# Sparse attention with its query and output projections woven between the head pairs, and sums of squares taken by piece before the last gated stage

## The reference, cut to what matters

```
qg = h @ w_qg
q = qg[:, :1024] * 64 ** -0.5;  gates = sigmoid(qg[:, 1024:])
o_cmp = softmax(q . k_cmp - slope * distance, visible) . v_cmp     # 15 compressed blocks
o_slc = softmax(q . k_slc - slope * distance, causal) . v_slc      # all 4 blocks are selected here
o_win = softmax(q . k_win - slope * distance, causal) . v_win
x = x + (g0 * o_cmp + g1 * o_slc + g2 * o_win) @ w_o
```

## Time and profile before

| what | value |
|---|---|
| median of 3 runs | 1021.89 us |
| the profiled execution's own time | 1023.04 us |
| its span, first to last instruction | 1021.2 us |
| granted TensorE clock, mean, as a share of full speed | 0.981 |
| PE busy | 976.2 us (96%) |
| DVE busy | 709.1 us (69%) |
| ACT busy | 483.9 us (47%) |
| chain that ended last | PE 82%, DVE 9%, ACT 5%, issue 2%, DMA 1% |

### The profile page before, as it was taken

One profiled execution on the slowest core, in us unless ns is written; L12 is line 12 of the kernel. 1 busy time (PEld: TensorE's weight loads), 2 busy tenths in 40 slices (PEclk: granted clock), 3 DMA queues, 4 the chain that ended last, 5 costly groups with the idle time before them and its releaser, 6 DMA issues.

```text
span 1021.2 us, 19481 instructions
## 1 busy us (share of the span) xinstructions
PE 976.2 (96%) x7934; PEld 945.4 (93%) x7934; DVE 709.1 (69%) x1128; ACT 483.9 (47%) x699; POOL 81.6 (8%) x129
## 2 busy tenths in 40 slices
PE   4999999999999998889999999999999789999998
PEld 4999999999999996569999999999999689999998
DVE  4876777777777646967777777677876466655554
ACT  5344634444445414866434444446757354444441
POOL 6000001000000011330010000011000000000000
PEclk9999999999999978999999999989999899999999
DMA  9655748687745670007668677543444254655531
GB/s 278 197 197 200 255 148 301 233 286 244 249 144 174 202 252 1 1 22 256 199 221 303 232 272 267 164 125 100 149 166 152 76 185 135 237 190 180 184 103 41
DMA packets 131387, 186.98 MB, mean 183 GB/s; under 512 B 6272, under 2 KB 102656, under 8 KB 131328
## 3 DMA queue, kind: packets, MB, share of 16 engines
q1 hardware_dynamic: 123984, 159.82, 47.2%
q0 software_dynamic: 6912, 25.17, 7.1%
q10 hardware_dynamic: 432, 1.16, 0.4%
HBM read 185.09 MB, written 1.05 MB: 182 GB/s over the span
## 4 chain that ended last, share of the span: by engine, by line
PE 82%; DVE 9%; ACT 5%; issue 2%; DMA 1%; SPq 0%; DVEq 0%; ACTq 0%
PE ps L1754 44%; PE ps L1823 15%; PE ps L1750 11%; PE ps L1752 3%; PE ps L1880 1%; DVE ada_acc L1156 1%; PE ps L1790 1%; DVE g_lo L1191 1%; ACT g_hi L703 1%; DMA g_raw<-in_a_w_in 1%; ACT g_hi L640 1%; ACT e_even L829 1%; DVE d_lo L1142 1%; DVE e_even L1436 1%; DVE g_lo L1091 1%
## 5 line engine op out<-in xcount | busy, mean ns | idle before, releaser
L1754 PE MATMUL ps<-opa_hi,g_hi 128*128 128x256 f32 x864 | 250.2, 290 | 14.8 <-DVE opa_lo L1128 11.9
L1754 PE MATMUL ps<-opa_lo,g_hi 128*128 128x256 f32 x864 | 247.3, 286 | 0.0
L1754 PE MATMUL ps<-opa_hi,g_lo 128*128 128x256 f32 x864 | 247.1, 286 | 0.0
L1754 PEld LDWEIGHTS ps<-opa_hi,g_hi 128*128 128x128 f32 x864 | 168.9, 195 | 17.8 <-issue 15.4
L1191 DVE TENSOR_TENSOR g_lo<-g_raw,g_hi 128x2048 fp32r<-128x2048 f32 x54 | 123.8, 2292 | 69.7 <-ACT g_hi L703 69.7
L1754 PEld LDWEIGHTS ps<-opa_lo,g_hi 128*128 128x128 f32 x864 | 168.8, 195 | 0.2
L1754 PEld LDWEIGHTS ps<-opa_hi,g_lo 128*128 128x128 f32 x864 | 168.7, 195 | 0.0
L1091 DVE TENSOR_TENSOR g_lo<-g_raw,g_hi 128x2048 fp32r<-128x2048 f32 x59 | 135.2, 2291 | 47.0 <-ACT g_hi L640 46.5
L640 ACT ACTIVATE g_hi<-g_raw 128x2048 fp32r<-128x2048 f32 x59 | 112.6, 1909 | 93.0 <-PE ps L1754 80.4
L1823 PE MATMUL ps<-hid_hi,d_hi 128*128 128x256 f32 x528 | 147.8, 280 | 1.5 <-issue 1.4
L1823 PE MATMUL ps<-hid_hi,d_lo 128*128 128x256 f32 x528 | 147.5, 279 | 0.0
(11 more groups left out here) (313 smaller groups left out, 1848.5 us busy)
## 6 DMA issues: line engine op xcount, KB each, us to landing
g_raw<-in_f_w_gu SPq DMA_DIRECT2D x44, 1024.0 KB, 8.9
ada_raw<-in_w_ada POOLq DMA_DIRECT2D x48, 512.0 KB, 5.2
d_raw<-in_f_w_down SPq DMA_DIRECT2D x22, 1024.0 KB, 5.2
g_raw<-in_w_in SPq DMA_DIRECT2D x14, 1024.0 KB, 7.8
g_raw<-in_w_gate SPq DMA_DIRECT2D x11, 1024.0 KB, 7.1
g_raw<-in_w_up SPq DMA_DIRECT2D x11, 1024.0 KB, 9.6
d_raw<-in_w_down SPq DMA_DIRECT2D x11, 1024.0 KB, 5.1
g_raw<-in_a_w_in SPq DMA_DIRECT2D x10, 1024.0 KB, 8.0
```

Of the source, the lines that this page charges most:

```text
L1754: mm = pe.matmul(pair(b)[:, a, :], wt[:, a * P:(a + 1) * P], xt, **st)
```

## The change

Query steps QG+2 and QG+3 and the output steps WO and WO+1 are cut into slices ("units") of six matmuls, and stand between the PE work of the head pairs. So `opb_hi` and `opb_lo` have to live through the attention, and `e_even` and `pt_buf` move to memory over the second half of `ada_acc`. Banks change: QG+2, QG+3 and WO use bank 6; the transposes of a pair rotate through banks 4 and 5 alone; the small products and `ada_sum(0)` use bank 7. The compressed attention is done in two halves of eight heads, the second one at pair 3. `ada_sum(0)` is cut in four and stands in front of `values(2)` to `values(5)`. DVE makes the low parts of QG+3 and WO, and takes the queries of QG+2 and QG+3, inside the attention. On ACT the high part of WO goes ahead of the exponentials of pair 3, and that of WO+1 ahead of those of pair 7. Ahead of the third feed-forward stage the squares are added piece by piece, all before the split of F2+1, and a Silu of two columns stands behind the root.

```diff
     def gbank(g):
-        return 4 + g % 4
+        return 6 if g in (QG + 2, QG + 3, WO) else 4 + g % 4
...
@@ ACT
             root((1, 3, 6)[f])
+            if f == 2:
+                act.activation(small[:, 12:14], eps[:, 0:2], ACT.Silu)
             split_g(g0 + 3)
...
-            split_g(WO)
...
+            compressed_exp(0)
             for j in range(1, NH // 2 + 2):
+                if j == 3:
+                    split_g(WO)
+                if j == 5:
+                    compressed_exp(1)
                 if j < NH // 2:
                     exps(j, 0)
...
-                        act.activation(pt_buf[:, 512 * q:512 * q + 512], ps[:, 4 + q, :], ACT.Copy).then_inc(pt_copied, 1)
+                        act.activation(pt_buf[:, 512 * q:512 * q + 512], ps[:, 4 + q % 2, :], ACT.Copy).then_inc(pt_copied, 1)
...
+                if j == 6:
+                    split_g(WO + 1)
...
+            squares(6, 3)
             split_g(F2 + 1)
-            squares(6, 3)
@@ DVE
             shift(0)
             shift(1)
+            own(dve.tensor_scalar(gates[:, :, :], gates[:, :, :], 1.0, None, ALU.add))
+            own(dve.reciprocal(gates[:, :, :], gates[:, :, :]))
+            compressed_shift(0)
             normalize(0)
             normalize(1)
...
+            compressed_factors(0)
+            evac_q(2)
+            split_g(QG + 3)
             for j in range(2, NH // 2 + 2):
                 for e in range(2):
                     if j < NH // 2 + 1:
                         normalize(2 * j - 2 + e)
+                    if j == 3 and e == 0:
+                        split_g(WO)
+                    if j == 4 and e == 0:
+                        evac_q(3)
                     if j < NH // 2:
                         shift(2 * j + e)
+                if j == 5:
+                    compressed_factors(1)
...
+                if j == 4:
+                    compressed_shift(1)
+                if j == 8:
+                    split_g(WO + 1)
...
+                if s in (2, 3):
+                    add_squares(6, (s - 1,))
+            add_squares(6, (3,))
             split_g(F2 + 1)
-            add_squares(6)
@@ PE
+            scores(0)
+            query_units(0, 2)
+            compressed_scores(0)
+            query_units(2, 1)
...
+            def turn(j, e):
...
+                        q = i // 4
+                        if i % 4 == 0 and (j >= 1 or q == 2):
+                            pe.wait_ge(pt_copied, 3 * j + 1 if q == 2 else 3 * j - q)
+                        mm = pe.transpose(ps[:, 4 + q % 2, i % 4 * P:(i % 4 + 1) * P], x[:, lo:lo + P], ident[:, :])
...
+                if 2 <= j < 6:
+                    ada_sum(0, 6 * (j - 2), 6)
...
+            scores(1)
+            pe.wait_ge(cs_shift, 1)
+            query_units(3, 2)
+            turn(0, 0)
+            query_units(5, 1)
+            turn(0, 1)
+            query_units(6, 2)
...
+            scores(2)
+            compressed_turn(0)
+            query_units(8, 1)
+            values(0)
+            query_units(9, 1)
+            turn(1, 0)
+            query_units(10, 1)
+            turn(1, 1)
+            query_units(11, 1)
...
+            out_units(0, 0, 2)
+            values(6)
+            out_units(0, 2, 1)
+            turn(7, 0)
+            out_units(0, 3, 1)
+            turn(7, 1)
+            out_units(0, 4, 2)
+            values(7)
+            out_units(0, 6, 1)
+            out_units(1, 0, 2)
+            out_units(0, 7, 1)
+            out_units(1, 2, 6)
+            for s in (2, 3):
+                g_step(WO + s, opa_hi, opa_lo, no_wait)
```

More of the change, by code:

```diff
@@ L175, in layer_kernel @@
     over = ExitStack()
+    sb("pad_e", [P, 3 * D], on=over)
+    e_even = sb("e_even", [P, 2, 768], on=over)
+    pt_buf = sb("pt_buf", [P, 1536], on=over)
+    over.close()
+    over = ExitStack()
     qk_a = sb("qk_a", [P, KT, T], on=over)
@@ L1926, in _ @@
             g_step(QG + 1, opb_hi, opb_lo, no_wait)
-            pe.wait_ge(gate_exp, 1)
-            for a in range(TT):
-                mm = pe.transpose(ps[:, 3, 256 + 48 * a:304 + 48 * a], gate_row[:, a * P:(a + 1) * P], ident[0:48, 0:48])
-            mm.then_inc(gate_turned, 1)
+            pe.wait_ge(g_evac, evacs(KV + 5))
             pe.wait_ge(cmp_hid_silu, 3)
@@ L1968, in values, with query_units @@
-            def values(j):
+            pe.wait_ge(gate_exp, 1)
+            for a in range(TT):
+                mm = pe.transpose(ps[:, 6, 256 + 48 * a:304 + 48 * a], gate_row[:, a * P:(a + 1) * P], ident[0:48, 0:48])
+            mm.then_inc(gate_turned, 1)
+            def query_units(first, n):
+                for u in range(first, first + n):
+                    s, k = QG + 2 + u // KT, u % KT
+                    if u == 0:
+                        pe.wait_ge(gates_copied, 1)
+                    if u == KT:
+                        pe.wait_ge(g_evac, evacs(QG + 2))
+                    g_step(s, opb_hi, opb_lo, no_wait, ks=range(k, k + 1))
@@ new lines, in out_units @@
+            def out_units(s, first, n):
+                for k in range(first, first + n):
+                    if s == 0 and k == 0:
+                        pe.wait_ge(pct_made, 2)
+                    if s == 1 and k == 0:
+                        pe.wait_ge(pt_copied, PT_NSA)
+                    g_step(WO + s, opa_hi, opa_lo, a_filled("attn"), ks=range(k, k + 1))
+            scores(0)
+            query_units(0, 2)
+            pe.wait_ge(kc_made, 4)
+            pe.wait_ge(g_evac, evacs(QG + 1))
@@ L1984, in values @@
                               start=False, stop=True, skip_group_check=True).then_inc(pv_done, 1)
-            for j in range(NH // 2 + 1):
-                if j + 1 < NH // 2:
-                    scores(j + 1)
-                if j == 0:
-                    pe.wait_ge(cs_shift, 1)
-                if j == 1:
-                    pe.wait_ge(cs_made, 1)
-                    for q in range(2):
-                        for a in range(TT):
-                            mm = pe.transpose(ps[:, 7, (2 * q + a) * P:(2 * q + a + 1) * P],
-                                              ctmp[:, a * T + q * P:a * T + (q + 1) * P], ident[:, :])
-                    mm.then_inc(pct_done, 1)
-                if j >= 1:
-                    values(j - 1)
-                if j < NH // 2:
-                    turn(j)
@@ new lines, in _ @@
+            turn(1, 1)
+            query_units(11, 1)
+            scores(3)
+            query_units(12, 2)
+            values(1)
+            query_units(14, 1)
+            turn(2, 0)
+            query_units(15, 1)
+            turn(2, 1)
+            pe.wait_ge(g_evac, evacs(QG + 2))
+            scores(4)
+            values(2)
+            turn(3, 0)
+            pe.wait_ge(g_evac, evacs(QG + 3))
+            compressed_scores(1)
+            turn(3, 1)
+            scores(5)
+            values(3)
@@ new lines, in _ @@
+            turn(4, 0)
+            turn(4, 1)
+            for j in (5, 6):
+                scores(j + 1)
+                if j == 5:
+                    compressed_turn(1)
+                values(j - 1)
+                turn(j, 0)
+                turn(j, 1)
+            out_units(0, 0, 2)
[7 more added lines that the diff above has]
+            out_units(0, 6, 1)
```

159 lines of the change are left out of this document (75 added, 84 removed).

## The result

The changed kernel takes 1013.70 us, the median of six runs (1011.51 to 1017.82), against 1022.12 us of the kernel before in the same session (1021.70 to 1026.34). The ratio is 0.9916, with a 95% interval of 0.9897 to 0.9935: faster by 8.6 us by the ratio (8.4 by the medians), where the forecast had said 14.9 and 1007.0 us, with 1002.5 to 1013.0 as its range. So the sign was right, the gain was put too high by 6.3 us, and the time lies 0.7 us above the range.

The account below looks back on a forecast made before the run. PE, busy 976.2 of 1021.2 us, was taken as the bound, with DVE bounding the attention's steady pairs; 11.0 us from the attention and 3.9 from the third stage made 14.9, giving 1007.0 us, range 1002.5 to 1013.0.

Parts of the forecast that it names:

- (a) to (c): Attention, first scores at 369.15 to DVE's loop at 389.1: one 3.1 us PE wait, one clock fall; lead 18.0.
- (d): Attention, DVE's loop from normalize(2) to normalize(14): 35.9 for six laps plus 8.5 of new work, 44.4 us; lead 10.7.
- (e): Attention's tail on PE, behind the copy at 434.0: 28.8 us, to 462.8, against 30.8 before; lead 12.2.
- handing over: Attention, some 15 new PE waits between engines: 0 to 3 us, taken as 1.2.
- third stage: Start of the third feed-forward stage: squares added earlier gain 2.6 us, earlier table load 1.3; 3.9 us together.
- PE keeps up: Attention, DVE's loop: PE's work there sums to 39.8 us, within the loop's 44.4.
- without slack: Behind the attention: WO+2's low part is ready as PE gets there, with no time to spare.
- the attention's 11.0 us: Whole attention: gain after its lead of 12.2 us less 1.2 for handing over.
- the second fall: Rival, attention pair 2: another clock fall behind PE's 1.7 us wait, 2.3 us on the path, 1009.3 us; chance 0.20.
- Two banks: Rival, attention pairs: turns wait for ACT's first copy, laps 9 us instead of 7.4, 1016.6 us; chance 0.06.
- The squares: Rival, third feed-forward stage: squares bring nothing because the additions delay the last piece, 1010.9 us; chance 0.06.
- fall in every pair: Rival, attention pairs: eight clock falls of 3.3 us, slower than before at 1026.9 us; chance 0.04.

Follow-up runs that it names:

- WO sooner: Changed kernel with ACT's high part of WO one pair earlier, ahead of pair 2's exponentials instead of pair 3's; 1008.78 us, 0.9866 of before.
- sums at the front: Changed kernel with the 24 column sums back in one block ahead of the compressed keys' products; 1018.49 us, 0.9956 of before.
- copy first: Changed kernel with ACT's copy of turn 0's first bank ahead of exps(1, 0) instead of behind it; 1010.69 us, 0.9877 of before.
- the three moves: Changed kernel with copy first, WO sooner and WO+1 sooner together; 1006.98 us, 0.9841 of before; second set 1007.63 us, 0.9849.
- WO+1 sooner: Changed kernel with ACT's high part of WO+1 between pair 4's first and second copy, not ahead of exps(7, 0); 1012.76 us, 0.9902 of before.
- sums in the wait: The three moves with 12 of 24 column sums put into PE's wait for QG+3's low part, the others in pairs 3 and 5; 1005.21 us, 0.9830 of before.

## Why the forecast was right in sign and too large

By its own steps, with the first profile of the changed kernel:

| step | forecast us | measured us |
|---|---|---|
| (a) to (c): first scores (370.40) to DVE's loop | 19.95 | 19.83 |
| (d): DVE's loop | 44.4 | 46.83 |
| (e), handing over included: to the end of WO+3 | 30.5 | 29.17 |
| third stage | gain 3.9 | gain 3.78 |

**(a) to (c) held**, with the mechanism named: the wait for ACT's copy (3.1 forecast, 2.85 measured), one fall of the clock behind it, QG+2's queries and the low part of QG+3 as DVE's last work ahead of the loop.

**(d) was too short by 2.4 us.** The wait for WO's high part is 2.95 and its low part 2.29, together 0.6 more than the 4.6 of the sum. The other terms (queries 0.68, compressed shift 1.25, factors 1.50) fit. What the sum lacked are three waits of 0.67, 0.93 and 0.95 us on PE and ACT (2.55; the six laps themselves took some 0.6 us less than the 35.9), of which the last hangs on WO+1's high part ahead of pair 7's exponentials. The sum had taken PE's total, 39.8, as proof that PE keeps up; it does so on average, and is late at single places. "WO sooner" shows that the wait for WO could have been spared: ACT stood idle one pair earlier.

**(e) was too long by 1.3**: the 1.2 us for handing over were not paid, and WO+2 waits 0.21 us, as "without slack" had it (the view puts this down to issue; the low part ends at 454.51, WO+2 begins at 454.61). So the step sums come out within 1.0 us (95.83 against 94.85), and the profile with neither the fall at QG nor the second one has a stretch of 117.84, where 128.37 less 11.0 is 117.37.

**What failed is the attention's 11.0 us: its base, and the falls of the clock.** The sum was made against one execution, and corrected by 1.15 us for the difference of the totals. In that execution the first fall behind QG+3, is longer than in the four other profiles of before; its stretch is 1.6 us over the mean of five. It made up for that elsewhere (its way from 523.20 to F2 at 822.47 takes 299.3 us, 300.6 in the second profile), so that its total was near the median while the stretch that the change removes was not. And the second fall, a rival with 0.20 at 2.3 us, came in three of six profiles; together with the fall at QG, which is on both sides, the changed kernel's mean lies 2.5 us over its best profile. From 11.0 that leaves 11.0 - 1.6 - 2.5 - 0.5 = 6.4, where 0.5 is what the steps themselves were out by (117.84 against 117.37), and the means give 6.5. This takes one difference apart and does not prove it again; the times do, with 5.7.

**The argument against the second fall was wrong in the forecast's own trace.** It was that PE would wait 1.7 us there, less than the 2.21 after which the clock fell. The same trace has a wait of 1.72 us at the first values, which the earlier trace rows leave out, and behind it a clock of 0.50, in the window that the earlier trace rows leave out:

```profile
409.64 2.83 PE L1979 MATMUL ps<-pt_buf,v_tok 128*64 128x256 f32 x16 [1.72 <-ACT gu L853]
```

```profile
409.75:413.05 3.30, 3.30 (x20) 2.25 (x20) 2.83 (x13) 1.80 (x8) 1.58 (x2) 0.50 0.00 0
```

The values take 2.83 us there in place of 1.52, and 2.08 to 2.83 in all five profiles of before. So a fall behind 1.7 us had been seen, and 0.20 was too little for it.

**The other rivals.** Two banks do not hold up the pairs: behind the first turn PE's waits for the copies are 0.25 to 0.91 us, and from the first shift of one lap to that of the next (402.79, 409.50, 417.26, 424.53, 431.60) DVE's loop takes 6.7 to 7.8 us, not 9. The squares do bring their part, 2.4 us; the 3.9 that the forecast put on this rival has the table load in it. The clock does not fall in every pair: 1.00 in the window from 408 to 414. The Trainium skill ("TensorE: Matmul & The Clock Gate", A second HAM failure mode) would have had it swing with the many short idle times between groups of matmuls; these runs show laps with such waits at 1.00, and single falls: behind waits of 2.85 to 2.87 or 2.51 to 2.53 us in each of the eleven profiles that have one, behind one of 1.61 to 1.64 and then 0.33 us in four of nine (three of the six of the changed attention, and sums at the front), and three times behind one of 0.84 or 0.85 (copy first, the second profile of the three moves, the changed kernel's third).

**One kernel's clock falls in one run and not in another.** The same scores behind the same waits of 1.61 and 0.33 us took 1.49, 2.57 and 2.27 us in the table above. The Trainium skill ("TensorE: Matmul & The Clock Gate", What's actually happening) states the like for the start of a kernel: the number of slow matmuls there is not the same in each run. The table shows it in the middle of one.

The forecast's own test, "the sum is wrong if the loop on DVE takes clearly more than 44 us, or if the clock is below 1.00 for more than one stretch", named both failures of the changed kernel. That its base might be off by as much, it did not ask.

## What to carry to other kernels

Where an engine's clock can fall in one run and not in the next, a stretch that a change removes is read from several profiles, or its steps are priced at the full clock and the falls apart; a total that is near the median says nothing on the stretch. Before a fall is argued away by the length of a wait, every wait of the trace at hand is held against the clock behind it. When work is moved into a loop that another engine bounds, ask for every wait in it where the late instruction could stand instead: an idle time of the engine that makes it, after its buffer is free. Here one index (pair 2 in place of pair 3) gave about as much as the change to the third stage (4.6 and 3.4 us, each known to some 2 to 4 us).

## What was not expected of the hardware

- In all six profiles that have the 24 products by one column in one block, the clock falls within it while PE is busy for all of the window: the block took 7.31, 8.26, 6.65, 7.18 and 8.22 us in the five profiles of before and 7.57 in "sums at the front", against 4 x 1.43 = 5.7 in quarters. No profile without the block has a fall at that place. 12 of the products in PE's wait were followed by the fall that the wait had had. What of a block makes it fall was not tried.
- The wait ahead of a fall does not decide alone. At QG waits of 0.90 and 1.76 us are followed by 7.44 us, waits of 1.20 and 1.28 by 5.91 and 5.92. In "sums at the front" no fall follows the first turn's wait of 2.14 us, and one follows the later wait of 1.61.
- Runs of one kernel spread by very different amounts: 6.9 us for the changed kernel over two sessions (twelve runs), 1.5 for "WO sooner" (five), 1.7 for "WO+1 sooner" and 1.6 for "sums at the front" (six each), 1.3 for "sums in the wait" (five). The waits left in a kernel do not order them; what does is open.
